# The dense attention without a constant matmul ahead of each value product

## The reference, cut to what matters

```python
def dilated_mixture(q, k, v, slopes):
    outs, lses = [], []
    for window, dilation in DILATED_CONFIGS:      # (128, 1), (512, 4), (2048, 16)
        o, lse = dilated_branch(q, k, v, window, dilation, slopes)
        ...
    alpha = jax.nn.softmax(jnp.stack(lses, 0), axis=0)
    out = jnp.sum(alpha[..., None] * jnp.stack(outs, 0), axis=0)
```

## Time and profile before

| What | Before |
|---|---|
| median of three runs | 4349.75 us (4335.72 to 4350.03) |
| span of the profiled execution | 4345.9 us |
| TensorE busy | 3757.2 us, 86% |
| weight loads busy | 2936.2 us, 68% |
| VectorE busy | 2014.9 us, 46% |
| ScalarE, GpSimd busy | 1094.3 us, 25%; 844.5 us, 19% |
| mean granted TensorE clock | 0.911 |
| dense attention in the trace | 2931.9 to 3204.6 us |

### The profile page before, as it was taken

The page is one execution under the profiler, slowest core; times in us unless marked ns, Lnnn a source line. Parts: engine busy times, 40 slices in busy tenths (PEclk is TensorE's granted clock), DMA queues, the critical chain, the costliest instruction groups (busy, mean ns, idle before and its releaser), DMA issues. The chain is left out here.

```text
span 4345.9 us, 43361 instructions
## 1 busy us (share of the span) xinstructions
PE 3757.2 (86%) x16633; PEld 2936.2 (68%) x16633; DVE 2014.9 (46%) x3149; ACT 1094.3 (25%) x1849; POOL 844.5 (19%) x621
## 2 busy tenths in 40 slices
PE   6968686979779887999999878989989969999997
PEld 5746465755568666888887365865668757777776
DVE  3254645216631323444444325877976343334344
ACT  3233233214222313121211014123435221111111
POOL 1046564000020002010100020000025132333243
PEclk9979797988889997999999969988999979999999
DMA  2012122100112101111111710100000211111111
GB/s 83 25 39 73 41 73 85 45 10 3 68 33 64 49 29 39 59 39 58 39 58 30 280 25 25 35 28 24 15 8 1 78 29 51 51 44 43 43 48 54
DMA packets 206820, 209.26 MB, mean 48 GB/s; under 512 B 13604, under 2 KB 147685, under 8 KB 206662
## 3 DMA queue, kind: packets, MB, share of 16 engines
q1 hardware_dynamic: 206662, 207.12, 15.2%
HBM read 198.70 MB, written 8.39 MB: 48 GB/s over the span
## 5 line engine op out<-in xcount | busy, mean ns | idle before, releaser
L185 PE MATMUL psum<-rounded,rounded 128*128 128x512 f32 (+2 forms) x4000 | 1573.3, 393 | 284.1 <-POOL rounded L770 86.0
L186 PE MATMUL psum<-rounded,rounded 128*128 128x512 f32 (+2 forms) x4000 | 1564.6, 391 | 0.0
L187 PE MATMUL psum<-rounded,rounded 128*128 128x512 f32 (+2 forms) x4000 | 1562.8, 391 | 0.0
L185 PEld LDWEIGHTS psum<-rounded,rounded 128*128 128x128 f32 x4000 | 774.2, 194 | 456.1 <-POOL rounded L770 90.8
L187 PEld LDWEIGHTS psum<-rounded,rounded 128*128 128x128 f32 x4000 | 773.6, 193 | 154.4
L186 PEld LDWEIGHTS psum<-rounded,rounded 128*128 128x128 f32 x4000 | 774.7, 194 | 150.9
L2015 POOL TENSOR_TENSOR plain<-plain,plain 128x512 f32<-128x512 f32 x176 | 248.4, 1449 | 533.1 <-DVE plain L2048 533.1
L370 POOL TENSOR_TENSOR rounded<-plain,rounded 128x512 fp32r<-128x512 f32 x100 | 140.6, 1418 | 717.1 <-ACT rounded L320 716.2
L2034 DVE TENSOR_TENSOR rounded<-plain,rounded 128x512 fp32r<-128x512 f32 x108 | 97.3, 901 | 321.4 <-ACT rounded L1957 321.3
L2630 POOL TENSOR_TENSOR plain<-plain,plain 128x128 f32<-128x128 f32 (+3 forms) x64 | 89.3, 1407 | 758.2 <-ACT plain L2701 737.0
L2059 DVE TENSOR_TENSOR plain<-psum,plain 128x512 f32<-128x512 f32 x44 | 30.4, 692 | 426.0 <-ACT plain L1968 426.0
(11 more groups left out here) (253 smaller groups left out, 4044.5 us busy)
## 6 DMA issues: line engine op xcount, KB each, us to landing
plain<-in_ff_w_dram SPq DMA_DIRECT2D x64, 512.0 KB, 5.0
plain<-in_w_ada_dram SPq DMA_DIRECT2D x12, 2048.0 KB, 20.1
plain<-in_w_gu_dram SPq DMA_DIRECT2D x44, 512.0 KB, 5.1
plain<-in_w_in_dram SPq DMA_DIRECT2D x36, 512.0 KB, 3.9
plain<-in_c_fwd_dram SPq DMA_DIRECT2D x64, 256.0 KB, 2.6
plain<-in_x_dram SPq DMA_DIRECT2D x3, 4096.0 KB, 15.2
plain<-in_w_down_dram SPq DMA_DIRECT2D x22, 512.0 KB, 3.7
plain<-in_c_inv_dram SPq DMA_DIRECT2D x32, 256.0 KB, 2.6
```

Of the source, the lines that this page charges most:

```text
L185: nc.tensor.matmul(out, wh, xh, start=first, stop=False)
L186: nc.tensor.matmul(out, wh, xl, start=False, stop=False)
L187: return nc.tensor.matmul(out, wl, xh, start=False, stop=last)
```

## The change

One call is taken out of `values`, for the dense stage. Everything else stays, the three constant matmuls at the start of the stage too.

```diff
                 elif not sparse and n >= 2:
                     pe.wait_ge(S["act_free"].sem, S["act_free"].at(n - 1))
-                if not sparse:
-                    keep_clock(core, 1, bank=6 + n % 2)
                 for j in range(i + 1):
```

## The result

The change makes the kernel slower: 4418.75 us median of four runs (4409.10 to 4429.29) against 4349.89 us (4335.72 to 4350.29), a ratio of 1.0176 with a 95% interval of 1.0144 to 1.0208 (the two medians alone give 1.0158). That it is slower is clear; whether by more than 2% is not. The forecast was 4424 us, within 4385 to 4445.

The account below looks back on a forecast made before the run. At full clock TensorE sets the dense stage's pace, VectorE 1.5 us per head behind; without constants, half clock makes TensorE alone the bound. Span 4345.9 + 74.6 = 4420.5 us, plus 3.85 gives 4424 us, range 4385 to 4445.

Parts of the forecast that it names:

- The clock: Dense stage without constants: granted clock 0.50 from beginning to end; half clock throughout given 0.70.
- the likeness: Dense-stage values and transposes, few columns per weight load, resemble records at 2534 to 2568 us, where clock stayed 0.50.
- the second rival: Dense-stage clock up for a part: 4391 us with 4 of 7 heads at half clock; range 4375 to 4408, chance 0.15.
- A head at half clock: Dense stage, TensorE: 38.6 us of work plus 8 x 0.35 us gives 41.4 us per head (41.1 to 42.4).
- the hand-over: TensorE time in each dense-stage pass beyond its matmuls: 0.31 to 0.47 us, taken as 0.35.
- The sum: Dense stage, first to last transposes: 321.5 us after against 246.9 before, 74.6 us more (72 or 82 by hand-overs).
- the apparent gain: TensorE time of the removed dense-stage constants at full clock: 6.8 us per head, up to 54 us.
- what VectorE lets through: Dense-stage gain when no score is late any more: 10.5 + (18.4 - 5.9), 23.1 us.
- The faster rival: Dense-stage clock stays up, VectorE's 27.0 us per head bound it: 4327 us; clock up 0.07, faster by over 0.5% 0.04.

Follow-up runs that it names:

- padded: Kernel after, no constants, with 128-row scores in the dense stage (queries copied by GpSimd beside zeros): 4335.6 us, ratio to before 0.9966.
- rows64: Kernel before with each of the 64 constant matmuls cut to 64 rows, columns unchanged: 4441.2 us in one run.
- opposite: Kernel before with 64-row constants always on the half of the rows the scores do not use: 4352.6 us, ratio to before 1.0019.
- after_c: The kernel after, unchanged, run again to catch one of its shorter runs: 4411.3 us, dense stage 311.7 us.
- double: Kernel before with two constant matmuls per pass in place of one: 4383.8 us in one run.
- heads4: Kernel before with constants only in heads 0 to 3, none in heads 4 to 7: 4383.4 us in one run.

## Why the prediction was right, step by step

*The clock.* Forecast: 0.50 from the beginning to the end of the stage. So it was in three of four profiled runs (apart from a few microseconds at either end), and up for 24 us of the fourth. The reason was that 64-row scores do not lift it, read from rows 7 and 8. Two pairs of runs show it directly, after against padded and rows64 against opposite: in each the columns are the same, the second puts the other 64 rows to work as well, and its clock is up for most of the stage.

*One argument in that step was wrong.* I took transposes and value products, with a weight load for few columns, for work that does not lift the clock either, by the likeness to the records at 2534 to 2568 us. The rise in after_c came behind just these, with 0.8 us of 64-row scores among 7 us of them. The clock also rose at 3270.7 us in the kernel after, in the last transposes and value products, 7.9 us behind the end of the last scores. The likeness failed. That the scores interrupt these stretches in every head is, I think, what kept the clock down and the forecast good, but no run tests it, and why one seam lifted the clock in one run and the same seams did not elsewhere stays open. It also makes the second rival, the clock up for a part, true in a small form: about one head in some runs. That is why the median of four runs, two near 4428 and two near 4410 us, lies 10.5 us below the profiled one, which was timed at 4429.29 us; that the two short runs had such a head is inferred from after_c. The nearness of 4418.75 to 4424 us is thus in part luck: 5.5 us too little for the stage stand against these shorter runs, which the sum did not have.

*A head at half clock.* Forecast 41.4 us within 41.1 to 42.4, measured 42.29. The columns were right: the pass at 3246.20 us has the durations of the earlier trace rows to 0.01 us, transposes and scores alike. The term that was mis-sized is the hand-over, 0.35 us per pass: the pass took 5.18 us, of which 0.85 + 2.56 + 1.29 are work, and 0.48 is left. I had let the 0.16 us between constant and first value record go with the constant. It did not: from the scores' end (3247.19 + 2.56) to the first value record are 0.30 us as before, and six value records then took 1.33 us to the next transposes where they took 1.17. The price moved from ahead of the first value record to behind it. padded shows what it hangs on: with scores of 128 rows the passes at half clock are 0.59 us shorter, which is the whole hand-over and more. In the pass of 2 transposes, 0.13 us of it lies between transposes and scores, 0.30 us between scores and values, 0.16 us in the values. So it belongs to the change between 64-row and 128-row matmuls; by what mechanism no run shows.

*The sum.* Forecast +74.6 us, with 72 to 82 by the hand-over; 80.1 us in the stage. With 0.46 us per pass the sum gives 38.6 + 3.7 = 42.3 us per head and 81.6 us; the first head was 0.9 us shorter than that (38.0 us without its missing value products), since the clock was up for its first 1.2 us.

*What the constants cost and bring.* At full clock a second one costs 0.85 us in full (double). I had 54 us as the apparent gain and 23.1 us as what VectorE lets through (the terms as shown add up to 23.0). padded shows what is to be had with the clock mostly up and no constants: 246.9 - 232.5 = 14.4 us. That is about the 23.1 us less the 9.8 us that VectorE still waits there.

*The faster rival* needed the clock to survive on short pauses. heads4 bounds it: without constants it survived some 20 us, and fell behind a pause of 1.31 us, 10 us ahead of the head's end. The rule of the Trainium skill that stands behind this rival ("TensorE: Matmul & The Clock Gate", section "Why this matters for your kernels") is not enough here: TensorE was busy for 320.00 of 320.00 us at half clock.

## What to carry to other kernels

A matmul without a use can be worth its time: here heads with 6.8 us of constants in them took 29.4 us, and 42.3 us without. Before one is taken out, ask what else in the stage keeps the granted clock up, and look at the rows of each matmul besides the engine's busy time. Better than a constant was here to make the useful work wide (the zeros beside a 64-row operand cost no TensorE time and saved 0.59 us of hand-over per pass at half clock), and once another engine is the bound, more clock brings nothing.

## What the runs showed of the hardware beyond that

Two 64-row float32 matmuls on different halves of the rows, issued one behind the other, ran side by side (starts 10 to 20 ns apart) without anything asked for, in rows64 by accident. On the same half each constant cost some 1.55 us of a pass at half clock. A pass of 64-row scores among 128-row matmuls took longer than the same pass with scores of 128 rows, by 0.59 us at half clock (19.44 against 17.09 us for four) and by 0.37 us at full clock (passes of 2 transposes, 1.65 us in after_c and 1.28 us in padded). And a dose of clock-keeping work can be worse than none and than the full one: 0, 256 and 512 columns gave 4419, 4447 and 4350 us.
